# Odd mixer of a two-block transformer kernel: q's norm factor moves into the exponential, and maxima, scalings and output products of the head pairs are issued in another order

## The reference

```
def odd_mixer(x, mix_norm, w_qkv, q_norm, k_norm, w_out):
    proj = rms_norm_2(x, mix_norm) @ w_qkv
    q, k, v = jnp.split(proj, [GQA_Q_WIDTH, GQA_Q_WIDTH + GQA_KV_WIDTH], axis=-1)
    q = rms_norm_2(q.reshape(Bsz, S, GQA_HEADS, GQA_HEAD_DIM), q_norm)       # 16 heads of 64
    k = rms_norm_2(k.reshape(Bsz, S, GQA_KV_HEADS, GQA_HEAD_DIM), k_norm)    # 4 heads of 64
    q = apply_rope(q, cos, sin)
    k = apply_rope(k, cos, sin)
    return gqa_block_attention(q, k, v) @ w_out      # softmax(q k^T / 8) v, then 1024 x 1024
```

## Time and profile before

| | |
|---|---|
| median of 3 runs | 1761.22 us (1759.41 to 1762.1) |
| the profiled execution | 1762.39 us, its span 1761.1 us |
| mean granted clock of TensorE | 0.968 of full speed |
| busy in the span | PE 94%, DVE 56%, ACT 45%, POOL 6% |
| the stage of the change | from 1449.31 us of the span to 1570.1 us |

### The profile page before, as it was taken

The page is one execution under the profiler, slowest core; times in us unless marked ns, Lnnn a source line. Parts: engine busy times, 40 slices in busy tenths (PEclk is TensorE's granted clock), DMA queues, the critical chain, the costliest instruction groups (busy, mean ns, idle before and its releaser), DMA issues. The chain is left out here.

```text
span 1761.1 us, 18639 instructions
## 1 busy us (share of the span) xinstructions
PE 1663.8 (94%) x7930; PEld 1357.7 (77%) x7930; DVE 981.4 (56%) x989; ACT 786.9 (45%) x953; POOL 100.2 (6%) x118
## 2 busy tenths in 40 slices
PE   6999998999999999989999998997899998599999
PEld 5877776788878888887888888775688886378887
DVE  4646675554474546665454556666545457644543
ACT  5444544444353434554343456433444444534442
POOL 1000100100010000001000000224000002000000
PEclk9999998999999999999999999977999999699999
DMA  8444541555455544543554453323365544025451
GB/s 325 186 185 174 191 156 48 193 189 191 169 190 193 200 184 178 197 166 120 191 195 187 176 194 122 119 61 88 127 220 186 191 185 153 1 96 218 188 191 48
DMA packets 51391, 289.36 MB, mean 164 GB/s; under 512 B 14023, under 2 KB 14791, under 8 KB 18026
## 3 DMA queue, kind: packets, MB, share of 16 engines
q1 hardware_dynamic: 50732, 286.87, 44.4%
q10 hardware_dynamic: 576, 1.29, 0.2%
HBM read 287.09 MB, written 1.05 MB: 164 GB/s over the span
## 5 line engine op out<-in xcount | busy, mean ns | idle before, releaser
L1752 DVE TENSOR_TENSOR wl<-raw,wh 128x2048 fp32r<-128x2048 f32 x260 | 588.8, 2286 | 177.9 <-ACT wh L1137 177.9
L513 PE MATMUL ps<-wh,xTh 128*128 128x512 f32 x1408 | 560.5, 398 | 20.1 <-DVE wl L1752 8.4
L513 PE MATMUL ps<-wh,xTl 128*128 128x512 f32 x1408 | 553.5, 393 | 0.0
L513 PE MATMUL ps<-wl,xTh 128*128 128x512 f32 x1408 | 553.2, 393 | 0.0
L1137 ACT ACTIVATE wh<-raw 128x2048 fp32r<-128x2048 f32 x260 | 489.0, 1907 | 2.7 <-PE ps L513 1.5
L513 PEld LDWEIGHTS ps<-wh,xTh 128*128 128x128 f32 x1408 | 267.6, 190 | 86.3 <-issue 10.1
L513 PEld LDWEIGHTS ps<-wh,xTl 128*128 128x128 f32 x1408 | 267.3, 190 | 57.3
L513 PEld LDWEIGHTS ps<-wl,xTh 128*128 128x128 f32 x1408 | 268.0, 190 | 54.1
L2439 POOL TENSOR_SCALAR st<-st 128x1 f32<-128x1 f32 (+2 forms) x46 | 30.3, 658 | 1452.7 <-ACT tmp L1156 850.5
L1200 ACT ACTIVATE sgf<-ps,st 128x256 f32<-128x256 f32 x22 | 10.5, 476 | 104.1 <-PE ps L513 104.1
L1200 ACT ACTIVATE sge<-ps,st 128x256 f32<-128x256 f32 x22 | 10.5, 476 | 99.5 <-PE ps L513 99.5
(11 more groups left out here) (329 smaller groups left out, 2328.6 us busy)
## 6 DMA issues: line engine op xcount, KB each, us to landing
raw<-in_w SPq DMA_DIRECT2D x260, 1024.0 KB, 4.8
gains<-in_rows SPq DMA_DIRECT2D x18, 512.0 KB, 4.1
x<-in_x ACTq DMA_DIRECT2D x2, 512.0 KB, 8.4
qn<-in_rpb SPq DMA_DIRECT2D x32, 32.0 KB, 2.5
xd<-in_rpb SPq DMA_DIRECT2D x32, 32.0 KB, 2.6
out_x<-x SPq DMA_DIRECT2D x2, 512.0 KB, 2.6
df<-in_cst SPq DMA_DIRECT2D x1, 368.0 KB, 23.4
tri<-in_cst SPq DMA_DIRECT2D x1, 320.0 KB, 6.1
```

The source lines that it names most:

```text
L513: return pe.matmul(o, lhs, rhs, start=start, stop=stop, skip_group_check=False)
L1752: TT(wl[:, p % RAW, :], raw[:, p % RAW, :], wh[:, p % RING, :].bitcast(F32), ALU.subtract).then_inc(*lo(p))
```

## The change

What it does, part by part:

- q is rotated straight out of PSUM, without its factor; ACT's squares go to a tile of their own (`od.sq`), and their sums are made behind the rotation. POOL writes the factors where the factor of a head is a pair of columns (`gqa_root`).
- `scores(i)` on DVE takes the maxima one head at a time and multiplies the two numbers by the head's factor (a new instruction for each head); ACT's exponential takes the factor as its scale.
- The two score banks are the same for every pair (4 and 5). A pair's two transposed halves share bank 6, and all value products bank 7. Each of them waits for what empties it.
- The order of all engines is written out. The output steps `out(q, t)` stand between the pairs: q is a piece, for which pairs 2q and 2q+1 have to be done, and both tiles of a piece follow each other.
- k's first rotation moves behind `turn_in("oddmix", 1)` and the gain tables; k's second rotation behind the one of `q_part(0, 1)`. All of `q_part(1, 1)` is before the second scores.
- The places of the splits of pieces are new.

```
-                emptied[s] = emptied[s + 1] = [(exped, tag, i, 1) if tag == "gqa" else (weighed, tag, i, 1)]
+            def gqa_turn_bank(j, t):
+                return 7 if j else 6 + t
 PE:
+                def scores(i):
+                    on.wait_ge(copied, "kTg", 1)
+                    on.wait_ge(copied, "qTg", i // 4, 1)
+                    for hh in range(2):
+                        clear(4 + hh)
...
+                        emptied[4 + hh] = [(exped, "gqa", i, hh)]
+                def keys():
+                    kv_turn(0)
+                    kv_turn(1)
+                    q_turn(0, 0)
...
+                q_part(0, 1)
+                q_part(1, 0, keys)
+                q_turn(0, 1)
+                q_part(1, 1, lambda: scores(0))
+                scores(1)
+                turn(0, 0)
+                q_turn(1, 0)
+                turn(0, 1)
+                scores(2)
+                turn(1, 0)
+                values(0)
+                turn(1, 1)
+                q_turn(1, 1)
+                scores(3)
+                turn(2, 0)
+                values(1)
+                turn(2, 1)
+                scores(4)
+                out(0, 0)
+                turn(3, 0)
+                values(2)
+                turn(3, 1)
+                out(0, 1)
+                scores(5)
+                turn(4, 0)
+                values(3)
+                turn(4, 1)
+                out(1, 0)
+                scores(6)
...
+                out(2, 0)
+                turn(7, 0)
+                values(6)
+                turn(7, 1)
+                out(2, 1, lambda: values(7))
+                out(3, 0)
+                out(3, 1, lambda: turn_in(AFTER["odd"], 0))
 ACT:
+                            e = act.activation(r.sc[:, i % 3, t, hh, :], bank(4 + hh)[:, 256 * t:256 * t + 256], ACT.Exp,
+                                               bias=r.sm[:, a + t:a + t + 1], scale=rr[:, t:t + 1], accum_out=r.sm[:, a + 2 + t:a + 3 + t])
...
+                ring.fill(2, p0 + 4)
+                scores(0)
+                q_stat(1, 1)
+                q_turn(1, 0)
+                scores(1)
+                turn(0)
+                scores(2)
...
+                turn(2)
+                ring.fill(1, p0 + 6)
+                values(1)
...
+                turn(4)
+                ring.fill(1, p0 + 7)
+                values(3)
 DVE:
+                def scores(i):
+                    for hh in range(2):
+                        a = 12 * (i % 3) + 6 * hh
+                        on.wait_ge(scored, "gqa", i, hh)
+                        dve.tensor_reduce(r.sm[:, a:a + 2], bank(4 + hh).rearrange("p (t n) -> p t n", t=2), AX.X, ALU.max, negate=True).then_inc(*made("peak", i, hh))
...
+                        TT(r.sm[:, a:a + 2], r.sm[:, a:a + 2], gqa_root(2 * i + hh), ALU.mult).then_inc(*peaked("gqa", i, hh))
...
+                q_rope(0, 1)
+                k_rope(1)
+                ring.fill(1, p0 + 2)
+                ring.need(p0 + 6)
+                ring.fill(1, p0 + 2)
+                q_rope(1, 0)
+                ring.fill(2, p0 + 4)
+                scores(0)
+                q_rope(1, 1)
+                scores(1)
+                scale(0)
+                scores(2)
+                scale(1)
+                values(0)
+                scores(3)
+                scale(2)
+                ring.fill(1, p0 + 6)
+                values(1)
+                ring.need(p0 + 10)
+                scores(4)
+                scale(3)
+                values(2)
+                ring.fill(1, p0 + 6)
+                scores(5)
+                scale(4)
+                ring.fill(1, p0 + 7)
+                values(3)
+                scores(6)
+                scale(5)
...
+                seam("odd", 0, p0 + 8)
+                ring.fill(1, p0 + 9)
+                turn_in(AFTER["odd"], 0)
```

More of the change, by code:

```diff
@@ new lines, in odd @@
+                out(0, 1)
[5 more added lines that the diff above has]
+                scores(6)
+                turn(5, 0)
+                values(4)
+                turn(5, 1)
+                out(1, 1)
+                scores(7)
+                turn(6, 0)
+                values(5)
+                turn(6, 1)
+                out(2, 0)
+                turn(7, 0)
+                values(6)
+                turn(7, 1)
@@ L1695, in q_turn @@
                     on.wait_ge(flipped, "qg", j, t)
[L1696 to L1704, removed]
+                    act.activation(od.qTg[:, 4 * j:4 * j + 4, 128 * t:128 * t + 128], halves(gqa_turn_bank(j, t)), ACT.Copy).then_inc(*copied("qTg", j, t))
@@ new lines, in turn, with values @@
+                def turn(i):
+                    for kk in range(2):
+                        on.wait_ge(turned, "gqa", i, kk)
+                        if i >= 2:
+                            on.wait_ge(valued, "gqa", i - 2)
+                        act.activation(r.PT[:, i % 2, kk, :, :], halves(6, 2), ACT.Copy).then_inc(*copied("gqa", i, kk))
+                def values(i):
+                    on.wait_ge(valued, "gqa", i)
+                    on.wait_ge(multiplied, p0 + 5)
+                    act.activation(xTh[:, i, :, :], bank(7)[:, 0:256].rearrange("p (t n) -> p t n", t=2), ACT.Copy).then_inc(*act_hi("ogqa", i))
@@ L1715, in odd @@
+                ring.fill(1, p0 + 2)
+                v_copy(1)
                 ring.need(p0 + 6)
[L1716 to L1725, removed]
@@ L1731, in scalar_program @@
+                values(3)
+                scores(6)
+                turn(5)
+                values(4)
+                scores(7)
+                ring.fill(1, p0 + 8)
+                turn(6)
+                values(5)
+                turn(7)
+                values(6)
+                values(7)
+                seam("odd", 0, p0 + 8)
+                ring.fill(1, p0 + 9)
+                turn_in(AFTER["odd"], 0, free=(tail, "odd"))
+                seam("odd", 1, p0 + 10)
             norm_stat("pre00", None, 0)
@@ L2401, in odd, with values @@
+                def values(i):
+                    on.wait_ge(act_hi, "ogqa", i)
+                    TT(xTl[:, i, :, :], bank(7)[:, 0:256].rearrange("p (t n) -> p t n", t=2), xTh[:, i, :, :].bitcast(F32), ALU.subtract).then_inc(*act_lo("ogqa", i))
                 ring.need(p0 + 2)
-                kv_part(0, p0)
+                ring.fill(1, p0)
+                turn_in("oddmix", 1)
+                tables_of_gains()
+                k_part(0)
                 ring.need(p0 + 4)
-                turn_in("oddmix", 1)
@@ new lines, in odd @@
+                scale(2)
+                ring.fill(1, p0 + 6)
+                values(1)
+                ring.need(p0 + 10)
+                scores(4)
+                scale(3)
+                values(2)
+                ring.fill(1, p0 + 6)
+                scores(5)
+                scale(4)
+                ring.fill(1, p0 + 7)
+                values(3)
+                scores(6)
+                scale(5)
+                values(4)
+                scores(7)
+                scale(6)
+                ring.fill(1, p0 + 8)
@@ L2418, in vector_program @@
+                values(5)
+                scale(7)
+                values(6)
+                values(7)
+                seam("odd", 0, p0 + 8)
+                ring.fill(1, p0 + 9)
+                turn_in(AFTER["odd"], 0)
+                seam("odd", 1, p0 + 10)
             pre_scale("pre00", None, 0)
```

199 lines of the change are left out of this document (130 added, 69 removed).

## The result

| | before | after |
|---|---|---|
| median of the runs | 1760.32 us | 1796.17 us |
| lowest to highest | 1759.28 to 1762.1 | 1788.53 to 1798.56 |
| profiled execution, its span | 1762.39, 1761.1 us | 1794.45, 1793.1 us |
| granted clock over the span | 0.968 | 0.961 |

The changed kernel takes 1.0191 times as long, with a 95% interval of 1.0176 to 1.0206. I predicted 1779, at most 1788: slower, as forecast, but twice as much.

A forecast was written before the change was run, and what follows sets the result against it. PE was taken as the bound, busy 94% of the span. Stage: 83.4 us of full-clock work + 45.8 of pauses + 9 of low clock = 138.2, against 120.8: +17.4, so 1779 us, range 1766 to 1788.

The forecast's parts named there:

- the ring: Attention: maxima, exponentials, copies, high and low part, scaling on DVE and ACT; 6.3 us a pair before, 8.5 with output step.
- The sum of the pauses: All PE pauses in the changed stage: 45.8 us, against 25.5 before.
- 1, middle of q_part(1, 0): PE waits for k's second rotation behind q_part(0, 1)'s, then for splits on ACT and DVE: 3.4 us.
- 2, scores(1): It writes to scores(0)'s banks, so waits for exponentials; DVE takes pair 0's maxima behind three splits and a rotation: 3.2 us.
- 3 and 4, turn(0, 0) and turn(0, 1): First waits for squares, rotation, maxima, scaling: 5.6 us; second shares bank 6, its copy late on ACT: 3.0 us.
- 5, behind five scores, pair 5's split included: Pairs 2, 3, 5, 6, 7: transposes wait for maxima and previous pair's scaling, 2.4 to 2.7 us each; split adds 1.6.
- 6, q_turn(1, 1): It waits in bank 7 for copy, high part and low part: 1.4 us.
- 7, out(0, 0), out(1, 0), out(2, 0): Splits ahead of a low part: out(0, 0) 3.2 us, out(1, 0) 5.1; split at turn(6) and the wait behind it 2.1.
- 8, turn_in and the next stage: Stage end: turn_in waits for out(3, 0)'s sum and gain, 1.3 us; next stage waits for its low part, 3.0.
- The entry: Stage start: the 3.29 us pause and 1.2 us of slow matmuls go; PE 4.9 us ahead, nearly used up by pause 1.
- The clock: Low clock after pauses in the stage costs 9 us, against 11.9 before; rival of 0 to 3 us had chance 0.24.
- the upper bound of 16: Clock loss if each of 16 listed pauses costs nearly 1.0 us on its first eight passes.

The follow-up runs named there:

- entry: Kernel before with only the changed kernel's entry: x's low part of the second tile ahead of gain tables and k's factor and rotation; 1761.16 us, ratio 0.9992.
- warm: Changed kernel with 182 extra idle transposes of the identity on PE, in ten of its pauses; 1780.19 us, ratio 1.0110 to the kernel before.

## Why the prediction was right or wrong

**Direction and mechanism: right.** Twelve output matmuls fill no more than their own place, PE waits inside the ring, and most waits are at the forecast places, ended by the forecast instructions.

**The sum of the pauses: right, 45.8 forecast and 46.2 measured, with errors that cancel.**

| pause | forecast | measured |
|---|---|---|
| 1, middle of q_part(1, 0) | 3.4 | 2.35 |
| 2, scores(1) | 3.2 | 2.64 |
| 3 and 4, turn(0, 0) and turn(0, 1) | 8.6 | 7.95 |
| 5, behind five scores, pair 5's split included | 14.5 | 17.15 |
| 6, q_turn(1, 1) | 1.4 | 1.51 |
| 7, out(0, 0), out(1, 0), out(2, 0) | 10.4 | 10.63 |
| 8, turn_in and the next stage | 4.3 | 3.98 |

Where I was short is point 5, "of which the second head's cover 0.5 to 0.8": they cover nothing, so each wait is 3.21. The small multiply, priced 0.2 by the reciprocal, takes 0.16, and the next instruction starts 0.08 us after its start; the reduction ahead of it takes 0.73 to the next start instead of 0.6, so the 1.6 us of the pair are right by two errors. The exponentials, priced 1.9 a pair, take 2.2; few waits hang on them.

**The entry: right as a pause that goes, and as a gain "nearly used up".** The run entry gives 0.9992 for it alone.

**The clock: wrong, and this is the step that failed.** "I take 9, a little over half of them: [...] of 2.4 to 2.7 many may pass." I set 83.4 us of full-speed work plus 9 against a stage that was at 83.4 + 46.2 + 22.1 = 151.7 us (from 1448.9 to 1600.57). Even the upper bound of 16 was short, and with it the range. Two things were wrong in it. I priced a low clock by its first eight passes, 1.0 us; but where 12 matmuls of 128x512 stand behind the pause, they stay at 1.2 GHz too, and out(0, 0) alone lost 2.4 us. By the count of the timeline the weight matmuls lost 8.7 us, which the forecast had nearly at nothing, and the short passes 10.7, close to its 9. And I let "many" pass, where 13 of the 16 pauses were followed by slow passes; of the five behind scores, four were, and they were 3.21 and 4.31 us, not 2.4 to 2.7. A third error isn't the clock: some 2.5 of the 22 us are the work itself, which takes 85.9 us and not 83.4 when it is broken up sixteen times. Filling the pauses bought back 10 us in the window, all of it where the output steps stand; what the slow passes that remain cost stays open.

**What I had right without using it:** "before, much of it lay beside the ring; now nearly each slow pass is on the path". The ring's pace of 6.3 us, the same at either clock, shows the first half, and warm the second, 10 us from 0.81 to 0.94. I should then have compared not 9 with 11.9, but a cost on the path with one that was mostly beside it.

## What to carry to other kernels

A low granted clock counts only where PE is on the path: test it by filling the pauses with idle transposes, and see in the timeline that these stand ahead of the wait and not behind it, since a null result can be a gain less their own time. When the change moves dense matmuls behind a wait, price the wait together with the matmuls behind it at half rate. A split that is moved away from one consumer can hand its pause to a later one, so cost it at both. Two executions of one program can differ by 3.7 us in a stage by the clock alone: compare pauses first, then time.

## What the runs showed that I had not expected

- The spread. The changed kernel's four runs go from 1788.53 to 1798.56 us, those of before from 1759.28 to 1762.1 (19 later ones from 1758.2 to 1764.92). The granted clock over the span is 0.968 in the fastest and 0.961, 0.958 and 0.959 in the others. The Trainium skill (TensorE: Matmul & The Clock Gate, Part 1) says that the number of slow matmuls at a kernel's start varies from run to run; here it varies in the middle too, and that with the slow matmuls on the path this becomes time is my reading of the four clocks.
- Behind one pause of 3.21 us the granted clock was 1.00, behind another of the same length 0.50 (the windows at 1564.13 and 1573.45). The length of the pause alone doesn't decide it.
- The maxima of the first head didn't start until the second head's scores had ended, though they wait for the first alone; that is so at pairs 2, 3, 6 and 7, where DVE was free. Why stays open.
